# Token columns moving instead of weight columns: the MLP up-projection of a two-block layer, with its output transposed

## The reference, cut to what matters

```python
h = rms_norm(x, g_mlp[l])                       # x: 256 x 2048
x = x + jnp.square(jax.nn.relu(h @ w_mlp_up[l])) @ w_mlp_down[l]
# w_mlp_up: 2048 x 8192, w_mlp_down: 8192 x 2048
# rms_norm: y = x * rsqrt(mean(x*x) + EPS), times g
```

## Time and profile before

| what | us |
|---|---|
| median of 3 runs | 2541.7 |
| lowest, highest | 2540.65, 2545.15 |
| the profiled execution: its own time | 2544.42 |
| the profiled execution: its span in the trace | 2542.3 |

### The profile page before, as it was taken

How to read it: one execution, slowest core, us unless ns; L and a number is a source line. 1 busy time by engine, 2 the same in 40 slices (tenths; PEclk the granted TensorE clock), 3 DMA queues, 4 the chain that set the end, 5 groups by cost and what they waited for, 6 DMA issues and landing times.

```text
span 2542.3 us, 31790 instructions
## 1 busy us (share of the span) xinstructions
PE 2460.7 (97%) x13402; PEld 2003.0 (79%) x13402; DVE 1581.6 (62%) x1515; ACT 1041.4 (41%) x863; POOL 264.5 (10%) x222
## 2 busy tenths in 40 slices
PE   7998999999999999999999999999999999999998
PEld 6777777787787888888888888887777777888786
DVE  6376457747677554554455457688999955446564
ACT  4444334433343444434434434444343444543342
POOL 0002100210000000000000000035555300000000
PEclk9999999999999999999999999999999999999999
DMA  6333344334665455555555555665555576566463
GB/s 241 126 133 117 125 142 157 118 126 153 246 232 188 175 190 190 185 195 183 197 183 192 188 202 204 222 233 194 188 198 191 188 258 232 169 235 230 191 226 141
DMA packets 83643, 475.42 MB, mean 187 GB/s; under 512 B 8640, under 2 KB 8768, under 8 KB 31808
## 3 DMA queue, kind: packets, MB, share of 16 engines
q1 hardware_dynamic: 83520, 473.64, 52.5%
HBM read 450.54 MB, written 23.07 MB: 186 GB/s over the span
## 4 chain that ended last, share of the span: by engine, by line
PE 82%; DVE 7%; DMA 5%; issue 3%; ACT 3%; SPq 0%; DVEq 0%; ACTq 0%
PE acc L1967 25%; PE acc L1969 24%; PE acc L1968 24%; DMA raw<-in_w 3%; PE banks L2123 3%; ACT w_hi L796 2%; DVE w_lo L1222 2%; PE banks L1978 1%; PE banks L2178 1%; DVE squares L1438 1%; DVE convT L1428 1%; DMA spilled<-stage 1%; PE banks L2265 1%; PE banks L2278 1%; PE banks L2078 1%
## 5 line engine op out<-in xcount | busy, mean ns | idle before, releaser
L1222 DVE TENSOR_TENSOR w_lo<-raw,w_hi 128x2048 fp32r<-128x2048 f32 x396 | 911.2, 2305 | 623.6 <-ACT w_hi L796 622.9
L796 ACT ACTIVATE w_hi<-raw 128x2048 fp32r<-128x2048 f32 x396 | 754.9, 1913 | 642.6 <-DMA raw<-in_w 642.4
L1967 PE MATMUL acc<-w_hi,a_hi 128*128 128x512 f32 x2112 | 850.2, 403 | 40.1 <-DVE w_lo L1222 31.6
L1968 PE MATMUL acc<-w_lo,a_hi 128*128 128x512 f32 x2112 | 829.9, 393 | 0.0
L1969 PE MATMUL acc<-w_hi,a_lo 128*128 128x512 f32 x2112 | 829.8, 393 | 0.0
L1967 PEld LDWEIGHTS acc<-w_hi,a_hi 128*128 128x128 f32 x2112 | 400.5, 190 | 149.0 <-DVE w_lo L1222 27.9
L1969 PEld LDWEIGHTS acc<-w_hi,a_lo 128*128 128x128 f32 x2112 | 400.5, 190 | 86.4
L1968 PEld LDWEIGHTS acc<-w_lo,a_hi 128*128 128x128 f32 x2112 | 401.1, 190 | 81.3 <-issue 1.9
L1967 PE MATMUL acc<-w_hi,b_hi 128*128 128x512 f32 x928 | 364.8, 393 | 0.0
L1969 PE MATMUL acc<-w_hi,b_lo 128*128 128x512 f32 x928 | 362.3, 390 | 0.0
L1968 PE MATMUL acc<-w_lo,b_hi 128*128 128x512 f32 x928 | 361.8, 390 | 0.0
(11 more groups left out here) (339 smaller groups left out, 1718.6 us busy)
## 6 DMA issues: line engine op xcount, KB each, us to landing
raw<-in_w SPq DMA_DIRECT2D x396, 1024.0 KB, 4.9
spilled<-stage SPq DMA_DIRECT2D x72, 256.0 KB, 6.0
gate_in<-spilled SPq DMA_DIRECT2D x20, 512.0 KB, 4.0
x_rows<-in_x SPq DMA_DIRECT2D x4, 512.0 KB, 9.7
x_rows<-in_x SPq DMA_DIRECT2D x1, 2048.0 KB, 10.6
mem_rows<-in_mem SPq DMA_DIRECT2D x2, 1024.0 KB, 4.8
spilled<-stage_b SPq DMA_DIRECT2D x8, 256.0 KB, 6.1
out<-y_rows SPq DMA_DIRECT2D x4, 512.0 KB, 2.8
```

Of the source, the lines that this page charges most:

```text
L796: act.activation(w_hi[:, n % HIGH, :], raw[:, n % RAW, :], ACT.Copy)\
L1222: dve.tensor_tensor(w_lo[:, n % RAW, :], raw[:, n % RAW, :], w_hi[:, n % HIGH, :].bitcast(F32), ALU.subtract).then_inc(lo_split, 1)
L1967: pe.matmul(o, hi[:, tk], wh, start=first, stop=False)
L1968: pe.matmul(o, hi[:, tk], wl, start=False, stop=False)
```

## The change: what it does

For `w_mlp_up` alone (`TURNED`) the operands of the product change places: a 128 x 128 square of the weights is stationary and the 256 tokens move. A unit is then 4 blocks x 4 squares x 3 = 48 matmuls of 256 columns. The result has the hidden columns on partitions: four groups of 128 lie in the two banks of `acc`, two to a bank. Relu writes them to `hidden`, now 128 x 8 x 256, without a scale. The step `hidden` has no part on PE and none of the `banks`: ACT squares `hidden` in place and rounds it to `b_hi`, DVE subtracts for `b_lo`. As relu(r x) squared is r squared times relu(x) squared, the factor moves to the residual add: DVE's add of each down chunk becomes a `scalar_tensor_tensor` with `rms("mlp", t)`, which now holds r squared, and `mlp_root` on ACT goes.

```diff
-        hidden = region("hidden", 0, [P, NT, W])
+        hidden = region("hidden", 0, [P, KW, T])
...
-                    (rows_src(hidden, t, 4 * j), b_dst(KW * (p % 2) + 4 * j, t), "square", None)
-                    for t in range(NT)]
+                    (hidden[:, 4 * j + 2 * g:4 * j + 2 * g + 2, :],
+                     [x[p % 2][:, 4 * j + 2 * g:4 * j + 2 * g + 2, :] for x in (b_hi, b_lo)], "square", None)
+                    for g in range(2)]
...
+                if mode == "square":
+                    act.activation(src, src, ACT.Square).then_inc(act_done, me.done(f"{tag}.{j}.tmp"))
+                    act.wait_ge(act_done, me.here())
+                    act.activation(dst[0], src, ACT.Copy).then_inc(act_done, me.done(f"{tag}.{j}.hi", f"{tag}.hi"))
+                    return
...
+            def hidden_in(p, j):
+                act.wait_ge(act_emptied, value(me, emptied(INDEX[("w_mlp_up", 2 * p + j)], "act"), 4 * NT))
+                jobs(f"hidden{p}.{j}")
...
-                        dst, func = hidden[:, t, (n % 2) * NW:(n % 2 + 1) * NW], ACT.Relu
+                        act.activation(hidden[:, 4 * (n % 2) + 2 * t:4 * (n % 2) + 2 * t + 2, :], src, ACT.Relu)\
+                            .then_inc(act_emptied, 1)
+                        continue
...
-                     "x_root": lambda: root("x", RMS["x"], NT), "mlp_root": lambda: root("mlp", RMS["mlp"], NT),
+                     "x_root": lambda: root("x", RMS["x"], NT), 
...
+                if mode == "square":
+                    dve.wait_ge(act_done, me.at(f"{tag}.{j}.hi"))
+                    dve.tensor_tensor(dst[1], src, dst[0].bitcast(F32), ALU.subtract)\
+                        .then_inc(dve_done, me.done(f"{tag}.{j}.lo", f"{tag}.lo"))
+                    return
...
+                        if name == "w_mlp_down0" and n == 0 and t == 0:
+                            dve.wait_ge(dve_done, me.at("mlp.inv"))
+                        if name == "w_o":
+                            ins = dve.tensor_tensor(x_rows[:, t, cs], x_rows[:, t, cs], src, ALU.add)
+                        else:
+                            ins = dve.scalar_tensor_tensor(x_rows[:, t, cs], src, rms("mlp", t), x_rows[:, t, cs],
+                                                           ALU.mult, ALU.add)
...
+                    if name in TURNED:
+                        for f in range(NW // P):
+                            fs = slice(f * P, (f + 1) * P)
+                            o = acc[:, i % 2, f // 2, f % 2 * T:f % 2 * T + T]
+                            pe.matmul(o, wh[:, fs], hi, start=u == 0 and k == 0 and f % 2 == 0, stop=False)
+                            pe.matmul(o, wh[:, fs], lo, start=False, stop=False)
+                            ins = pe.matmul(o, wl[:, fs], hi, start=False, stop=u == units - 1 and k == KU - 1 and f % 2 == 1)
+                        continue
...
             def hidden_jobs(p, j):
-                pe.wait_ge(act_emptied, value(me, emptied(INDEX[("w_mlp_up", 2 * p + j)], "act"), 4 * NT))
-                jobs(f"hidden{p}.{j}")
+                pass
```

More of the change, by code:

```diff
@@ L79 @@
 CHUNKS = weight_chunks()
+TURNED = ("w_mlp_up",)
 INDEX = {(c[0], c[1]): i for i, c in enumerate(CHUNKS)}
@@ L806, in job @@
                     return
+                if mode == "square":
[3 more added lines that the diff above has]
+                    return
                 k = ts_turn[0] % 2
                 ts_turn[0] += 1
[L809 to L817, removed]
+                act.wait_ge(dve_done, me.at(f"{tag}.{j}.tmp"))
                 act.activation(dst[0], four(ts[:, k, :]), ACT.Copy)\
@@ L846, in empty @@
                 act.wait_ge(pe_used, value(me, FIRST[i + 1], LOOP_UNITS))
-                norm = "x" if i <= INDEX[("w_gate_a", 3)] else "mlp" if name == "w_mlp_up" else \
-                    "mem" if name.startswith("xa_w") else "pre"
+                norm = "x" if i <= INDEX[("w_gate_a", 3)] else "mem" if name.startswith("xa_w") else "pre"
                 if n == 0 and me.it is None:
-                    ready = {"w_f": "x.rinv", "w_mlp_up": "mlp.rinv", "xa_wv": "mem1.rinv"}.get(name)
+                    ready = {"w_f": "x.rinv", "xa_wv": "mem1.rinv"}.get(name)
                     if ready:
@@ L1062, in _ @@
                      "pre_root": lambda: root("pre", RMS["pre"], NT),
-                     "hidden": lambda p, j: jobs(f"hidden{p}.{j}"),
+                     "hidden": hidden_in,
                      "ssm_small": ssm_small, "ssm_u": ssm_u, "ssm": ssm,
@@ L1080, in slot_work @@
                 run_steps(me, steps, 2 * n + 1)
-            def after_loop():
-                ts_user[:] = [f"hidden{NPIECE - 2}.1.0"] * 2
-            drive(me, slot_work, after_loop)
+            drive(me, slot_work, lambda: None)
             root("out", RMS["out"], NT)
@@ L1232, in job @@
                     return
+                if mode == "square":
[3 more added lines that the diff above has]
+                    return
                 k = ts_turn[0] % 2
                 ts_turn[0] += 1
[L1235 to L1240, removed]
+                if ts_user[k]:
+                    dve.wait_ge(act_done, me.at(f"{ts_user[k]}.hi"))
+                dve.wait_ge(pe_done, me.at(f"{tag}.{j}.T"))
+                dve.tensor_tensor(four(ts[:, k, :]), four(bank_of(tag, j)), g, ALU.mult)\
+                    .then_inc(dve_done, me.done(f"{tag}.{j}.tmp"))
                 dve.wait_ge(act_done, me.at(f"{tag}.{j}.hi"))
-                if mode == "gain":
-                    dve.wait_ge(dve_done, me.here())
+                dve.wait_ge(dve_done, me.here())
                 dve.tensor_tensor(dst[1], four(ts[:, k, :]), dst[0].bitcast(F32), ALU.subtract)\
@@ L1351, in empty @@
                             dve.wait_ge(loaded["x2"], 16)
-                        ins = dve.tensor_tensor(x_rows[:, t, cs], x_rows[:, t, cs], src, ALU.add)
+                        if name == "w_mlp_down0" and n == 0 and t == 0:
[5 more added lines that the diff above has]
+                                                           ALU.mult, ALU.add)
                     elif name == "glu_w":
@@ L2358, in slot_work @@
                 run_steps(me, steps, 2 * n + 1)
-            def after_loop():
-                last_use[:] = [f"hidden{NPIECE - 2}.1.0.hi"] * 4
-            drive(me, slot_work, after_loop)
+            drive(me, slot_work, lambda: None)
 def chunk_of(st, d):
```

## The result

The change made the kernel slower by half a per cent: 2556.45 us median of 5 runs (2554.52 to 2559.38), against 2541.7 (2540.65 to 2545.83). The ratio is 1.0052 with the interval 1.0041 to 1.0063, outside what can't be told from no change. The forecast was 2527.0, with 2548 as the upper end. The profiled execution has its own time of 2554.52 and a span of 2552.7 us, at the same granted clock of 0.989. Of all executions in this document one, of experiment 9, took 11222 us for no known reason, and its ratio leaves it out.

The account below looks back on a forecast made before the run. PE, busy 97% of the span, was taken as the bound. Profiled 2544.4 - 15.9 (transposes) + 1.2 (width) = 2529.7 us; that execution being 2.7 above the median, the forecast was 2527.0, range 2524 to 2548 for 8 in 10.

Parts of the forecast that it names:

- The width: Up-projection on PE: 1536 matmuls of 512 columns become 3072 of 256 at 0.1137 us a step, +1.2 us.
- rival 1: Up-projection on PE: each load stalls the stream 13.3 ns, step 120.4 ns, net +5.9 us, 2547.6 us; chance 14%.
- both at once: PE matmuls: 128-column loads and 128 columns moving in two passes overlap fully, 0.1115 us a step instead of 0.21.
- the rule of the Trainium skill: PE: a load overlaps a running matmul only in another row group; step 0.223 us, product +338 us; prediction rejected it.
- rival 4: Hidden step: DVE or ACT holds back a split, PE waits about a microsecond in each of sixteen, about 2543; chance 4%.
- The transposes: Sixteen hidden steps on PE: removing the transposes of `hidden` saves 15.9 us.
- ACT, DVE, DMA and what stands behind: MLP and later stages: other engines' changed work stays hidden by PE, counted 0; stages behind equally long, only earlier.
- rival 3: Up-projection on PE: the weight load isn't hidden, +235 to +338 us, so 2745 or more; chance 3%.

Follow-up runs that it names:

- experiment 9: Kernel before with weights stationary in the up-projection, eight 512-column then eight 256-column matmuls, no transposes, loop written out: 2538.41 us against 2543.04, ratio 0.998.
- experiment 5: Changed kernel with 24 more matmuls of one shape behind each of 48 up-projection blocks, sixteen settings; only steps read, 120.0 ns for 128 stationary, 256 moving.
- experiment 2: Changed kernel with its hardware loop of 3 turns written out as straight code: 2548.47 us, ratio to before 1.0018.
- experiment 1: Changed kernel with 512-column steps and operands back in their old places, still without transposes: 2526.62 us against 2543.36 for before, ratio 0.9931.
- experiment 4: Kernel before with each 512-column up-projection matmul split in two of 256, operands in old places, transposes kept: 2580.46 us, ratio 1.0147.

## Why the prediction was wrong

- **The width, the step that failed.** "The settled step is half of 0.2267, so the stream costs by the column", and from it 0.1137. It was 0.1200: 3072 x 0.0063 = +19.4 us of the 29.5 by which the forecast missed. The number in the earlier trace rows was right, and experiment 5 finds 113 to 118 ns again for 32 stationary columns. Carrying it to 128 stationary columns was the error. One row of another shape agreed with half of a wide step, and I took the agreement for a law. The prediction's own rival 1 had the right number, 120.0, and a chance of 14%; its time, 2547.6, is still 8.9 us short, which is the loop. What spoke against it there, "32 loaded columns should then stall less than a quarter of it", argued against one mechanism and not against a fixed part of 13.3 ns; that mechanism fits only some of the shapes of experiment 5.
- **The bound "both at once"** held: 128 columns moving go at 111.7 ns with loads of 128 columns to all rows. It told that the load is not added, but not that nothing else is. By the rule of the Trainium skill that the prediction told of ("TensorE: Matmul & The Clock Gate"; it stands in the section "The mechanism", not in the one that the prediction names), experiment 5 would show load and stream added, 165 ns at 128 moving columns (111.7 + 128/2.4); the trace disagrees.
- **The loop, not in the prediction at all.** 384 more matmuls a turn of the loop, 768 instructions with their loads, were counted as time on the array and never as code. 7.9 us by the gaps and 1.3 by the lower clock behind them; 8.0 by the medians in experiment 2. No row of before shows this cost, but its trace has the branch of 0.24 us and no packet of instructions in the second and third turns, which say that the loop lives where it needn't be fetched; I didn't ask how near its edge it was. The "new wait" of rival 4 was sought on ACT and DVE. The wait came on PE's own instruction stream.
- **The transposes** were right: 15.9 us worked out, 16.7 by the medians (13.5 to 21.9 by the interval of the ratio) in experiment 1.
- **ACT, DVE, DMA and what stands behind** were right: PE waited for none of them, and the time after the MLP was 1.1 us less.
- **A slip in rival 3.** 2541.7 - 15.9 + 235 is 2761, not 2745. Nothing hangs on it.
- **The sum again with what was measured:** 2527.0 + 19.4 + 7.9 + 1.3 = 2555.6, against 2556.45. The executions of each kernel spread over 5 us, so that it closes to 1 us is in part luck.

The placing of the operands, which the change is about, had no price of its own. What decided were two things that it brought along: half as many columns behind each load, and a longer loop.

## What to carry to other kernels

Price a matmul by its own pair of shapes, stationary and moving: where a row for the pair is missing, a step of another stationary width is a bound and not a value, and here 6 ns on 3072 matmuls outweighed all that was removed. Count what a change does to the number of instructions in a hardware loop, engine by engine, and look at the branch's time in the trace; near the edge, writing the loop out may cost nothing that can be told, as it did here. An idle gap on PE can cost more than its length: look at the granted clock behind it. When the profile names a releaser for a new wait, ask whether the same instruction stood there before without one.

## What the runs showed of the hardware that was not expected

- float32r matmuls with a 128-column load each: 111.7 ns for 128 and 192 moving columns, then 120.0, 146.7, 173.3, 202.5 and 226.7 for 256 to 512 in steps of 64, at the 2.4 GHz level of the clock. It makes no difference whether a new square or the same one is loaded, or which tensor stands.
- Narrow loads help at 256 moving columns (116.0 with 96, 113.3 with 64) and hurt at 512 (229.7 with 64, 231.6 with 32, against 226.7). Open.
- Alternating 512 and 256 columns costs 353.2 ns a pair, groups of eight 349, where 346.7 is the sum of each alone. Behind 256-column matmuls the first five 512-column steps are 228 to 236 ns and only the sixth is settled, in experiments 5 and 9 alike. Why is open.
- A hardware loop whose body on PE has 1654 instructions turns in 0.24 us, one of 1780 in 5.7 to 5.8 us; a turn then holds PE up for 3 to 7 us in two gaps. The edge lies between these counts of this kernel's mixture of instructions; it wasn't narrowed further, nor tried on another engine, nor with a long loop of 512-column matmuls alone.
- The granted clock fell to 0.50 behind such gaps: between the two gaps of the second turn of the changed kernel (14 steps of 0.214 us for 0.120), behind the second gap of each turn of experiment 4 (29 steps), and not at the first turn of the changed kernel, though its gaps are of the same size.
